# Expert layer in 32-row tiles, four runs side by side on TensorE's column groups

## The reference

```python
eid = gi[:, None] * EXPERTS_PER_GROUP + ti            # 2 experts of 16 for each token
comb = jnp.sum(jax.nn.one_hot(eid, N_EXPERTS) * tw[..., None], axis=1)
hg = jnp.einsum('nd,edf->nef', t, w_eg)               # d = 1024, f = 256
hu = jnp.einsum('nd,edf->nef', t, w_eu)
a = jax.nn.silu(hg) * hu * comb[..., None]
out = jnp.einsum('nef,efd->nd', a, w_ed)
x = _layernorm(ALPHA * x + (1.0 + g2) * out, ln2_g, ln2_b)
```

## Time and profile before

| what | us |
|---|---|
| median of 3 runs | 2109.7 (2105.01 to 2111.42) |
| profiled execution: span, the only time of it that the page gives | 2103.6 |
| experts: first gate/up matmul to the start of the last down | 1558.5 to 2011.8 |
| from there to the end (last store, `combine`) | 91.8 |

### The profile page before, as it was taken

How to read it: one execution, slowest core, us unless ns; L and a number is a source line. 1 busy time by engine, 2 the same in 40 slices (tenths; PEclk the granted TensorE clock), 3 DMA queues, 4 the chain that set the end, 5 groups by cost and what they waited for, 6 DMA issues and landing times. The chain is left out here.

```text
span 2103.6 us, 30608 instructions
## 1 busy us (share of the span) xinstructions
PE 1718.4 (82%) x11079; PEld 1064.3 (51%) x11079; DVE 732.0 (35%) x1167; ACT 431.1 (20%) x755; POOL 285.6 (14%) x392
## 2 busy tenths in 40 slices
PE   5999998789886988888599999799448898789920
PEld 3444446444444656555399999644224343344410
DVE  2110119344553433343354554254421111111138
ACT  1000011244432222222043343101101111011113
POOL 0000010100002111110032231022300000000034
PEclk8999999777777999999699999999769989899965
DMA  8323420000005999999354545521059878879944
GB/s 309 116 101 103 162 85 3 1 1 0 0 0 172 385 387 387 387 387 387 109 141 120 143 115 134 191 87 70 26 199 313 280 255 283 290 258 325 306 156 155
DMA packets 276134, 385.44 MB, mean 183 GB/s; under 512 B 18220, under 2 KB 175549, under 8 KB 276054
## 3 DMA queue, kind: packets, MB, share of 16 engines
q1 hardware_dynamic: 262904, 336.85, 47.7%
q0 software_dynamic: 8560, 30.97, 4.3%
q10 hardware_dynamic: 4608, 16.78, 2.0%
HBM read 354.48 MB, written 30.07 MB: 183 GB/s over the span
## 5 line engine op out<-in xcount | busy, mean ns | idle before, releaser
L2097 PE MATMUL ps<-we_w_gu,ex_xT 128*128 128x512 f32 x512 | 256.2, 659 | 57.0 <-DMA we_w_gu<-w_exp_up 55.4
L326 PE MATMUL ps<-w_w,g_arena 128*128 128x512 f32 x512 | 228.4, 605 | 7.6 <-issue 4.0
L2097 PEld LDWEIGHTS ps<-we_w_gu,ex_xT 128*128 128x128 f32 x512 | 106.8, 212 | 202.9 <-issue 200.6
L1503 PE MATMUL ps<-mix_x_hi,mix_w_hi 128*128 128x352 f32 x576 | 188.7, 328 | 18.5 <-DVE mix_x_lo L1467 16.8
L1503 PE MATMUL ps<-mix_x_hi,mix_w_lo 128*128 128x352 f32 x576 | 186.9, 324 | 0.0
L1503 PE MATMUL ps<-mix_x_lo,mix_w_hi 128*128 128x352 f32 x576 | 186.5, 324 | 0.0
L1133 PE MATMUL ps<-g_ident,sat_k_pg 128*128 128x128 f32 x1024 | 129.0, 280 | 42.7 <-DMA sat_k_pg<-cache_k 38.7
L326 PEld LDWEIGHTS ps<-w_w,g_arena 128*128 128x128 f32 x512 | 97.6, 193 | 127.2 <-issue 125.9
L1133 PEld LDWEIGHTS ps<-g_ident,sat_k_pg 128*128 128x128 f32 x1024 | 113.9, 144 | 75.6 <-issue 70.1
L1545 DVE TENSOR_TENSOR mix_w_lo<-mix_w_raw,mix_w_hi 128x1024 fp32r<-128x1024 f32 x73 | 125.9, 1756 | 32.9 <-ACT mix_w_hi L1530 25.0
L1102 ACT COPY sat_kT<-ps 128x512 f32<-128x512 f32 x128 | 73.5, 587 | 249.7 <-PE ps L1133 249.7
(11 more groups left out here) (371 smaller groups left out, 2140.7 us busy)
## 6 DMA issues: line engine op xcount, KB each, us to landing
sat_k_pg<-cache_k SPq DMA_DIRECT2D x256, 256.0 KB, 7.9
sat_v_pg<-cache_v SPq DMA_DIRECT2D x256, 256.0 KB, 7.9
we_w_gu<-w_exp_gate SPq DMA_DIRECT2D x32, 1024.0 KB
we_w_gu<-w_exp_up SPq DMA_DIRECT2D x32, 1024.0 KB
we_w_dn<-w_exp_down SPq DMA_DIRECT2D x32, 1024.0 KB, 8.3
mix_w_raw<-w_in SPq DMA_DIRECT2D x49, 512.0 KB
g_arena<-w_ada SPq DMA_DIRECT2D x16, 1024.0 KB
y_rows<-ex_y ACTq DMA_DIRECT2D x32, 512.0 KB, 6.8
```

Of the source, the lines that this page charges most:

```text
L326: last = nc.tensor.matmul(ps[:, b, :], g.hT[:, k, t * P:(t + 1) * P], w[s][:, k, :], start=(k == 0), stop=(k == KD - 1))
L1503: last = nc.tensor.matmul(out, w[p][:, at], v[:, x, :], start=(i == 0 and k == 0), stop=(i == len(w_chunks) - 1 and k == 2))
L2097: last = nc.tensor.matmul(ps[:, 2 + s, :], xT[s][:, k, :], w_gu[s][:, k, :], start=(k == 0), stop=(k == KD - 1))
```

## The change

Tiles have 32 slots instead of 128. A routing needs at most 81 of them; they are dealt into four runs of `STEPS` = 21 consecutive tiles each, and one step works on the four tiles that stand at the same place in the four runs. Their rows lie side by side in the 128 rows of a step, run `c` at rows 32c to 32c+31. TensorE multiplies each run's 32 rows by that run's own weights, into that run's 32 partitions of PSUM, that is on its own group of 32 columns of the array. Each run has one buffer for its weights, four in all, and a run's weights are loaded only where its expert differs from that of the step before (a flag beside the owner, `dma_start(cond=...)`). Gate/up loads are split into two halves of the 1024 rows, gate on SP and up on ScalarE's queue. The row weight (`slot_weight`, from a second series of matmuls in `route`) is multiplied in with the product of the activations, so `combine` only adds. POOL issues the gathers and the stores; the engines' loops are written out.

```diff
+TR = 32
+RUNS = P // TR
+SLOT_TILES = (2 * T - NEXP) // TR + NEXP
+STEPS = -(-SLOT_TILES // RUNS)
...
+STEP_TILES = (T + TR - 1) // TR
+WIDE = STEPS + STEPS % 2
...
                 pe.wait_ge(placed, 2)
                 for n in range(2 * NT):
-                    last = nc.tensor.matmul(ps[:, 2, 0:SLOT_TILES], at_row[:, n, :], token_in_tile[:, n, :],
+                    last = nc.tensor.matmul(ps[:, 2, 0:WIDE], at_row[:, n, :], token_in_step[:, n, :],
...
+                pe.wait_ge(placed, 3)
+                for n in range(2 * NT):
+                    last = nc.tensor.matmul(ps[:, 3, 0:WIDE], at_row[:, n, :].bitcast(F32), weight_in_step[:, n, :],
...
+                v.tensor_tensor(g.tile_expert[:, 1:STEPS, :, 1], by_run[:, 1:STEPS, :], by_run[:, 0:STEPS - 1, :],
+                                ALU.not_equal).then_inc(have_experts, 1)
...
+    def load_gate_up(self, eng, owners, src, at, half, arrived):
+        k = slice(half * KD // 2, (half + 1) * KD // 2)
+        for c, (e, other) in enumerate(owners):
+            eng.dma_start(self.gate_up[c][:, k, at:at + DE],
+                          src[bass.ds(e, 1), :, k, :].rearrange("a p k f -> (a p) k f"), **other).then_inc(arrived[half], 16)
...
+    def load_first(self, sp):
+        owners = self.owners(mybir.EngineType.SP, 0)
+        for half in range(self.HALVES):
+            self.load_gate(sp, owners, half)
+            self.load_up(sp, owners, half)
+        self.load_down(sp, owners)
...
+                for i in range(1, STEPS):
+                    owners = weights.owners(mybir.EngineType.SP, i)
+                    for half in range(HALVES):
+                        sp.wait_ge(half_used[half], i)
+                        weights.load_gate(sp, owners, half)
+                    sp.wait_ge(y_full, i)
+                    weights.load_down(sp, owners)
...
+                gather(0)
+                gather(1)
+                for i in range(STEPS):
+                    if i + 2 < STEPS:
+                        gather(i + 2)
+                    store(i)
...
+                    for half in range(HALVES):
+                        pe.wait_ge(xT_copied[half], i + 1)
+                        pe.wait_ge(weights.gate_in[half], 16 * RUNS * (i + 1))
+                        pe.wait_ge(weights.up_in[half], 16 * RUNS * (i + 1))
+                        for k in range(half * KD // 2, (half + 1) * KD // 2):
+                            for c, at in runs:
+                                last = nc.tensor.matmul(ps[at, 2 + s, :], xT[s][:, k, at], w_gu[c][:, k, :], start=(k == 0),
+                                                        stop=(k == KD - 1))
+                        last.then_inc(half_used[half], 1)
...
+                    if i + 1 < STEPS:
+                        gate_up(i + 1)
+                    a_transposes(i)
+                    if i + 2 < STEPS:
+                        x_transposes(i + 2)
+                    down(i)
...
+                    if i + 2 < STEPS:
+                        owners = weights.owners(mybir.EngineType.Activation, i + 2)
+                        load_up(owners, 0, i + 2)
+                    if i + 1 < STEPS:
+                        silu(i + 1)
+                    if i + 2 < STEPS:
+                        copy_x(act, copy, 1, i + 2)
+                        load_up(owners, 1, i + 2)
+                    copy_y(act, copy, 1, i)
...
-                    nc.vector.scalar_tensor_tensor(out=r_t[b][0:rows, :], in0=yb[b][0:rows, :],
-                                                   scalar=g.weight[0:rows, 1, t:t + 1], in1=ya[b][0:rows, :],
-                                                   op0=ALU.mult, op1=ALU.add).then_inc(added[b], 1)
+                    nc.vector.tensor_tensor(r_t[b][0:rows, :], yb[b][0:rows, :], ya[b][0:rows, :], ALU.add)\
+                        .then_inc(added[b], 1)
```

More of the change, by code:

```diff
@@ L2005, in __init__, with owners @@
         self.down_v = io["w_exp_down"][0].rearrange("e (k p) n -> e p k n", p=P)
[L2007 to L2018, removed]
+    def owners(self, engine, i):
+        row = self.g.tile_expert[0:1, i].rearrange("a c n -> a (c n)")
+        values = self.nc.values_load_multi_w_load_instructions(
+            row, engines=(engine,), min_val=0, max_val=NEXP - 1,
+            skip_runtime_bounds_check_because="experts and flags are worked out on the chip")[1]
+        return [(values[2 * c], {"cond": values[2 * c + 1]} if i else {}) for c in range(RUNS)]
@@ L2021, in experts @@
 def experts(nc, io, g, ps, weights):
     KE = DE // P
-    LAST = SLOT_TILES // 2 - 1
+    HALVES = weights.HALVES
+    runs = [(c, slice(TR * c, TR * c + TR)) for c in range(RUNS)]
     with ExitStack() as ctx:
@@ L2058, in _ @@
             def _(sp):
-                with sp.Fori(1, LAST + 1) as use:
-                    for s in range(2):
-                        weights.load(sp, 2 * use + s, s, (gu_full[s], START + use), (y_full[s], START + use))
+                for i in range(1, STEPS):
[5 more added lines that the diff above has]
+                    weights.load_down(sp, owners)
@@ L2115, in down @@
                         for k in range(KE):
-                            last = nc.tensor.matmul(ps[:, 6 + half, :], aT[s][:, k, :],
-                                                    w_dn[s][:, k, half * 512:(half + 1) * 512], start=(k == 0),
-                                                    stop=(k == KE - 1))
-                    last.then_inc(y_full[s], 1)
-                x_transposes(0, 0)
-                gate_up(0, 0)
-                x_transposes(0, 1)
-                with pe.Fori(0, LAST) as use:
-                    for s in range(2):
-                        gate_up(use + s, 1 - s)
-                        a_transposes(use, s)
-                        x_transposes(use + 1, s)
-                        down(use, s)
@@ L2130, in _ @@
[L2130 to L2144 removed]
+                            for c, at in runs:
+                                last = nc.tensor.matmul(ps[at, 6 + half, :], aT[s][:, k, at],
+                                                        w_dn[c][:, k, half * 512:(half + 1) * 512], start=(k == 0),
+                                                        stop=(k == KE - 1))
@@ new lines, in down, with copy_x @@
+                    last.then_inc(y_full, 1)
+                x_transposes(0)
+                gate_up(0)
+                x_transposes(1)
+                for i in range(STEPS):
+                    if i + 1 < STEPS:
[4 more added lines that the diff above has]
+                    down(i)
+            def copy_x(eng, copy, half, i):
+                s = i % 2
+                eng.wait_ge(xT_full[half], i + 1)
+                copy(xT[s][:, 4 * half:4 * half + 4, :], ps[:, half, :].rearrange("p (k n) -> p k n", k=4))\
+                    .then_inc(xT_copied[half], 1)
@@ L2206, in _, with silu, load_up @@
-                for s in range(2):
-                    act.wait_ge(stored[s], START + 16 * (LAST + 1))
+                def silu(i):
+                    s = i % 2
+                    act.wait_ge(half_used[HALVES - 1], i + 1)
+                    if i >= 2:
+                        act.wait_ge(a_done, i - 1)
+                    nc.scalar.activation(gate[s][:], ps[:, 2 + s, 0:DE], ACT.Silu).then_inc(gated, 1)
+                def load_up(owners, half, i):
+                    act.wait_ge(half_used[half], i)
+                    weights.load_up(act, owners, half)
@@ L2387, in hybrid_decoder_step @@
             weights = ExpertWeights(nc, io, g, Mem(nc, w_ctx, "we"))
-            route(nc, io, g, ps, weights.load)
+            route(nc, io, g, ps, weights.load_first)
             experts(nc, io, g, ps, weights)
```

301 lines of the change are left out of this document (149 added, 152 removed).

## The result

The changed kernel takes 2117.0 us (median of 20 runs, 2113.89 to 2122.97), the kernel before in the same session 2106.3. The ratio is **1.005, interval 1.0035 to 1.0066**: slower by half a per cent, where 1957 us had been forecast. The profiled execution spans 2116.0 us against 2103.6.

A forecast was written before the change was run, and what follows sets the result against it. TensorE and the transfers were both taken as near the limit in `experts`. 2103.6 - 165 (`experts` 292 instead of 457) + 13.5 (start) - 1.2 (`combine`) = 1951, plus 6.1: 1957 us; own range 1935 to 1990, whole range 1920 to 2015.

The forecast's parts named there:

- Weights of a run that changes: In `experts`: reloads into the single buffer land near 2.5 and 7.2 us, needed at 4.8 and 8.4, so hidden.
- C: Rival in `experts`: reloads miss their window and the clock falls, 18.5 us a step with a reload, 2013 us; chance 0.13.
- TensorE's work of a step, 12.1: In `experts`: gate/up 7.3 us, down 3.65 and transposes 1.1, with the four column groups working at the same time.
- D: Rival in `experts`: the four streams hinder each other, 0.14 instead of 0.114 us an instruction, 2009 us; chance 0.02.
- E: Rival in `experts`: weight loads not hidden behind another group's matmul, 0.112 us more an instruction, 2183 us; chance 0.02.
- Quiet step 12.4, with a reload 14.3, together 264: Transitions in `experts`: 6 without reload at 12.4 us, 12 with one at 14.3, one double at 18, sum 264.
- rival B: In `experts`: POOL's chain to the gather rules every step, 14.9 us each, 1980 us; chance 0.16.
- Skipped loads at nothing: In `experts`: issues of skipped loads, at most 3.6 us on ScalarE and 5.4 on SP, fit in 12, cost nothing.
- The start, +13.5: Longer `route` and more loads to issue put the first gate/up at 1572, 13.5 us later; bounds +10 and +17.
- The two last downs, 9.5 as before: End of `experts`: the last two down matmuls take 9.5 us, as in the kernel before.
- `combine` -1.2: In `combine`: 1.16 us of ScalarE on the first tile goes, so 1.2 us less.
- The 6.1 by which the median lies above the span: Whole kernel: 6.1 us added to the summed span of 1951 to get the median, 1957 us.

The follow-up runs named there:

- e1: The changed kernel with SP issuing the gate loads of step i+1 ahead of the down loads of step i; 1969.6 us, ratio 0.931.
- e3: The kernel of e1 with all 14 reloads left out, every flag of a changed expert at zero; 1915.3 us.
- e5: The kernel of e1 with POOL issuing the gather of step i+3 ahead of the store of step i; 1947.3 us, ratio 0.925.
- e8: The changed kernel with SP's order as it was and only POOL's gathers moved ahead of the stores; 2117.7 us.
- e2: The changed kernel with all 14 reloads left out, every load issued and skipped, SP's order as it was; 2018.8 us.

## Why the prediction was wrong

**The step that failed** is the bullet "Weights of a run that changes". It took the gate loads as issued when their half of the buffer comes free, -3.65 us from the end of gate_up(i+1): "the changed run's pair (gate on SP, up on ScalarE) is issued at -2.4". That is nearly so for ScalarE's queue. On SP the gate loads of step i+2 stand behind the down loads of step i+1, and these wait for down(i), which ends at +4.8, the very moment at which gate_up(i+2) could start. The wait was in the diff (`sp.wait_ge(y_full, i)` ahead of `load_down`, in the same loop), and I had asked whether SP's issues fit into a step (5.4 us of 12), not what stands ahead of them. The runs showed 155.6 us of waits for `w_exp_gate` in its place, and transitions of 414.4 us where 264 had been summed. e1 mends that one thing and brings 1969.6, 13 us from the forecast and within its range. Of the rivals none was this: C (the window missed, the clock falling) had the symptom, 18.5 us a reload where the 12 steps with one reload took 23.8 on average, but as a matter of bytes, and it left the quiet steps alone; the six took 15.6, 17.4, 18.4, 17.4, 18.0 and 18.2.

**The other steps:**
- *TensorE's work of a step, 12.1.* Right: 11.7. 64 instructions take 7.05 us, 0.110 each, with their weight loads. D and E are out. The Trainium skill's rule that weight loads overlap only with matmuls on other rows of the array (TensorE: Matmul & The Clock Gate, section Part 3: Packing small matmuls) does not hold for these four column groups: a load alone takes 0.110 us in the median and 0.128 in the mean, so 0.110 for load and matmul together leaves no time for loads that stand by themselves.
- *Quiet step 12.4, with a reload 14.3, together 264.* With the order mended 272.3 (e1), but that the sum is so near is in part luck, since the split was wrong: the six quiet transitions took 14.7 us on average and the twelve with one reload 13.9. In e1 what a reload delays is the gather, and TensorE meets that wait also in the quiet step behind it, 32.6 us in 11 waits. So rival B's chain (down, copy, store, gather) was real, but not in every step, as B had it: the gather's median to landing was 7.2 us in e1 against 4.6 in e3, where no loads run beside it. With that mended too, the transitions take 245.3 (e5), and four of the six quiet ones 11.7.
- *Skipped loads at nothing.* Right with the order mended: 0.073 us for the issue itself and some 0.24 to 0.45 with the register work around it, and e3's step holds nothing but TensorE's work. In the changed order they are part of the 4 us that each quiet step waits.
- *The start, +13.5.* Measured +16.8, within the bounds. SP's last issue in `route` ended at 1564.4, which fits the limit by bytes (1565) and not the one by packets (1558).
- *The two last downs, 9.5 as before.* Too low: down(20) waits 6.2 us for its own reload, issued after down(19), and runs at the low clock after it. The stretch from the start of gate_up(20) took 26.2 us instead of 16.8.
- *`combine` -1.2.* Measured -2.1. But from the end of the last down to the first work of `combine` it is 9.3 us instead of 4.9, a term that was left out. The last store is issued 1.2 us after the end of the last down on POOL, 0.8 on ScalarE's queue before; what fills the other 4 us no run shows.
- *The 6.1 by which the median lies above the span.* Every run here is 1.7 to 1.8 us longer than its own span (2117.72 and 2116.0 in the changed kernel's profiled one); the rest is spread between runs. The median of all 20 runs of the kernel before, 2106.3, lies 2.7 above the span, which puts the forecast at 1954.

Put together: start +16.8, `experts` -6.8, from the last down to `combine` +4.4, `combine` -2.1: +12.3 of the 12.4 between the spans.

## What to carry to other kernels

Read the order of every queue as a chain of waits: for each load, ask which wait stands last ahead of it in program order, not only when its buffer is free. With single buffers that question decided this case, since nothing is fetched ahead to cover a late issue; a wait for the end of a step in front of the loads for the next step puts the whole transfer in the open. When a mended wait uncovers the next one (here the gather), an edit for the second is worth nothing before the first is made (e8), and 27 us of the transitions after (e5). And a total of waits over a window can hold a wait that is none of the loop's: look at the timeline for where each one stands.

## What the runs showed of the hardware

- Four column groups with float32 data of their own work at once almost without loss: 0.110 us for a 32-column matmul instruction of 512 elements with its weight load, against 0.43 for a full-width one, a factor of 3.9.
- A load skipped by its flag moves nothing and signals all the same (e2 runs on with every load skipped, and a reload adds its whole 3.15 MB); its issue takes 0.073 us on SP and 0.09 on ScalarE's queue, against 0.37 for a real load on SP and 0.34 for a store on ScalarE's queue before.
- The page's memory-read figure counts issued loads: 512.29 MB with 0, 14 and 80 reloads, while the queues moved 286, 330 and 538 MB.
- In e2 TensorE waits some 4 us in each step, and gate/up behind it takes 8.4 to 8.8 us instead of 7.05: the granted clock is 0.50 (1.2 GHz) when it starts and back at 2.4 within it. So a step lost 1.3 us or more beyond its wait. The windows of e2 behind the wait that ends at 1703.7 (columns as in the earlier trace rows):

```profile
1704.00:1706.00 2.00, 2.00 (x12) 0.45 (x8) 0.00 (x0) 0.00 (x0) 0.00 (x0) 0.50 0.89 246
1706.00:1712.00 6.00, 6.00 (x56) 1.71 (x48) 0.00 (x0) 0.00 (x0) 0.00 (x0) 0.93 0.02 8
```
